# Last overflow tile of the expert stage finished apart from the other rows of a one-core decoder layer

## The chip, the cores and the metric

The kernel runs on one core of one Trainium2 chip. The metric is device time in microseconds (us), and the median of three runs before the change is 911.37 us (910.29 to 911.94). One further execution was recorded by the hardware profiler. It took 905.44 us, of which 903.5 us lie between its first and its last instruction; this stretch is called the span. All times in the tables and rows below come from that one profiled execution.

## The reference

One decoder layer over 1024 positions of width 1024: four kinds of token mixing and an output projection, then a mixture of experts with 32 experts of which each row uses two, then a plain residual add and a final RMSNorm. Only the end matters here:

```python
y = jnp.concatenate([ya, yb, yc, yd.astype(x.dtype)], axis=-1) @ w_out[l]
x = x + gt1 * y
h2 = rms_norm(x, norm2_g[l]) * (1.0 + sc2) + sh2
x = x + gt2 * hier_moe(h2, ...)       # per row: sum of two experts' outputs, each with its gate
...
return rms_norm(x, final_g)           # x * rsqrt(mean(x*x) + 1e-6) * final_g
```

An output row can be normalised only once both of its expert results are in its sum.

## The kernel before, in words

**Where the sums live.** The residual rows `x + gt1 * y` are stored in DRAM as `y_d` (1024 rows of 1024 floats, 4 KB each), and the rows that the experts read are stored as `xn2_d`. Each expert takes at most 128 rows. The table `tbl` holds, for each tile of work, a column with the row numbers of its 128 places; a place that isn't used has a number beyond the last row, and the indirect transfer leaves it out.

**Tiles.** Tiles 0 to 31 are the 32 experts in a fixed order. Rows that don't fit into their expert's 128 places go to overflow tiles 32, 33, ..., whose count `n_ov` is read from memory at run time (at least 1). With these inputs it is 1, so tile 32 is the only overflow tile. Each tile is gathered from `xn2_d` (GpSimd, `fetch`, L705), transposed by TensorE (`ex_t`), modulated by VectorE and ScalarE (`modulated`), multiplied with gate and up weights (`ex_gu`), passed through the activation (`hidden`), multiplied with the down weights (`ex_dn`), scaled by its gate into a result buffer `yo` (VectorE, `result`, L2140), and added to `y_d` by an indirect DMA that accumulates (GpSimd, `scatter_add`, L711). There are three result buffers (tile e uses `yo[e % 3]`); the overflow tile uses `yo[0]`.

**GpSimd around the end (L734 to L770).** After the scatter of tile 31 it gathers tile 33, which has no rows and is only there because each turn of the loop fetches one tile ahead. It reads `n_ov`, waits for all scatters to land (`s_sc`), and enters the overflow loop: copy the row numbers into `idx`, wait for VectorE's result (`m_yd`), start the scatter of tile 32, wait for TensorE's transposes of the next tile (`m_tx`), gather again, wait for the scatter to land, raise `ov_go`. Behind the loop it raises `f_go`.

**SyncE (L528 to L535).** It waits for `f_go`, then issues eight loads of 512 KB that bring `y_d` back into `x1[:, 0]` to `x1[:, 7]`, then eight stores to the output, each as soon as its rows are normalised (`f_o`).

**The final norm.** ScalarE squares and sums each of the eight tiles (L1356, from the last loop of its program), VectorE adds epsilon for two tiles at a time (`root_args`, L2175), GpSimd raises that to the power -0.5 (L770), and VectorE multiplies rows, factor and `final_g` (L2183, one instruction for each tile). VectorE runs `root_args` of the next pair ahead of the multiplications of a pair.

The order of the work is written out by hand; each engine runs its list in order and waits on semaphores.

Of the kernel before, what the change touches and what calls it, by code (L numbers as in the profile page):

```python
# [12 lines left out]
ALU = mybir.AluOpType  # L13
ACT = mybir.ActivationFunctionType
AX = mybir.AxisListType
ds = bass.ds
# [5 lines left out]
NT = T // P  # L22
# [92 lines left out]
def build(nc, w, out):  # L115
    ctx = ExitStack()
    with ctx:
# [3 lines left out]
        def sem(name):  # L121
            return ctx.enter_context(nc.semaphore(name))
# [126 lines left out]
        ac, o = area(REG_Y, o, 2, P)  # L249
        assert o == RES_END and o + D <= 8 * D  # L250
        fg = gtb[:, 0]

        o = RT
        rt = {}
# [89 lines left out]
        def identb(n):  # L344
# [17 lines left out]
                 "rt_pos  rt_hot far_ld rt_ld rt_n "  # L362
                 " m_tx m_xa m_xd m_gu m_th m_act m_dn m_yd "
                 "ov_w "
                 "rt_c rt_e1 rt_e2 rt_oh f_go ov_go st_x1 f_ss f_o").split()
        s = {n: sem(n) for n in names}
        s_ada = [sem(f"ld_ada{i}") for i in range(4)]
        s_win = [sem(f"ld_win{i}") for i in range(2)]
# [4 lines left out]

            return 48 * n + (16 if u >= RING - NT // 2 else 0)

        s_gx = [sem(f"gathered{i}") for i in range(BUF)]
        s_sc = [sem(f"scattered{i}") for i in range(RES)]
        s_st = [sem(f"st_xn2_{i}") for i in range(2)]
        s_fo = sem("st_out")
# [160 lines left out]
        def _(gp):  # L540
# [170 lines left out]
            def scatter_add(at, b):  # L711

                gp.indirect_dma_start(out=y_d[:, :], out_offset=bass.IndirectOffsetOnAxis(ap=at, axis=0),  # L713
                                      in_=yo[b], in_offset=None, bounds_check=last_row,
                                      oob_is_err=False, compute_op=ALU.add).then_inc(s_sc[b], 16)
# [18 lines left out]
            for e in range(3):  # L734
                gather_behind(e)
            for e in range(E):
                gp.wait_ge(s["m_yd"], e + 1)
                scatter_add(rows_of(TURN[e], 0), e % RES)
                gather_behind(e + 3)
                if e == E - 1:  # L740
                    gp.wait_ge(s["m_tx"], E + 1)
                    gather(E + 1, 0)
                if e + BUF == E:
                    gp.wait_ge(s["far_ld"], 32)
                    gp.wait_ge(s["m_tx"], E - BUF + 1)
                    gather(E, 0)
                if e == 2:
                    gp.wait_ge(s["rt_n"], 2)
                    gp.wait_ge(s["far_ld"], 16)
                if 2 <= e < 2 + 2 * NT:  # L750
                    far_scatter(e - 2)
                if e == E - 5:
                    gp.sem_inc(s["ov_go"], 1)
            n_ov = gp.value_load(idy[0:1, 0:1], min_val=1, max_val=OVT)
            for b in range(RES):
                gp.wait_ge(s_sc[b], 16 * len(range(b, E, RES)))
            with gp.Fori(0, n_ov) as i:
                ch.enter(i, 4)
                scatter_add(rows_of(i + E, 1, i + (E + 1)), 0)
                gp.wait_ge(s_gx[0], i * 16 + 16 * (E // BUF + 2))  # L760
                at = rows_of(i + (E + 2), 0, count=i + (E + 2), done="m_tx")
                fetch(at, 0)
                gp.wait_ge(s_sc[0], i * 16 + 16 * (len(range(0, E, RES)) + 1))
                gp.sem_inc(s["ov_go"], 1)
            gp.sem_inc(s["f_go"], 1)

            for i in range(NT // 2):
                gp.wait_ge(s["f_ss"], i + 1)
                at = slice(2 * i, 2 * i + 2)
                gp.tensor_tensor(rs[:, 2, at], ss[:, 2, at], mhalf[:, 0:2], ALU.pow).then_inc(s["rstd_ready"], 1)  # L770

        @block.tensor
# [580 lines left out]
        def _(act):  # L1354
# [261 lines left out]
            for j in range(NT):  # L1616
                act.wait_ge(s_w[j], w_loads(j, len(range(j, E, RING))) + 16)
                if j >= 2:
                    act.wait_ge(s["ss_ready"], 2 * NT + j - 1)
                fn(fsq[:, j % 2], x1[:, j], ACT.Square, scale=ROOT, accum_out=ss[:, 2, j:j + 1]).then_inc(s["ss_ready"], 1)  # L1620

        @block.vector
        def _(dve):
# [513 lines left out]
                stt(ac[:, par, :], a1[:, par, :], 0.5, PS[2 + par][:, P:2 * P], ALU.mult, ALU.mult).then_inc(s[pre + "act"], 1)  # L2138

            def result(e, par, pre="m_"):  # L2140
                b = e % RES if isinstance(e, int) else 0
                dve.wait_ge(s[pre + "dn"], e + 1)
                if isinstance(e, int) and e >= RES:
                    dve.wait_ge(s_sc[b], 16 * (e // RES))
                for h in range(2):
                    last = stt(yo[b][:, h * 512:(h + 1) * 512], PS[4 + 2 * par + h][:, :], gate(TURN[e] if isinstance(e, int) else e), gtb[:, 1, h * 512:(h + 1) * 512],  # L2146
                               ALU.mult, ALU.mult)
                last.then_inc(s[pre + "yd"], 1)
# [14 lines left out]
            with dve.Fori(0, n_ov) as i:  # L2163
                ch.enter(i, 1)
                hidden(i + E, 0, free=False)
                dve.wait_ge(s_sc[0], i * 16 + 16 * len(range(0, E, RES)))
                result(i + E, 0)
                modulated(xt[:, 0], i + (E + 2), "m_tx", "m_xd", 1)

            dve.wait_ge(s["xr_ld"], 16 * (NT + 1))  # L2170

            def root_args(i):
# [5 lines left out]
            for i in range(NT // 2):  # L2178
                if i + 1 < NT // 2:
                    root_args(i + 1)  # L2180
                dve.wait_ge(s["rstd_ready"], 2 * NT + i + 1)
                for j in (2 * i, 2 * i + 1):
                    stt(x1[:, j], x1[:, j], rs[:, 2, j:j + 1], fg, ALU.mult, ALU.mult).then_inc(s["f_o"], 1)  # L2183
# [24 lines left out]
```

## Time and profile before

| what | value |
|---|---|
| median of three runs | 911.37 us |
| profiled execution | 905.44 us, span 903.5 us |
| TensorE busy | 845.6 us, 94% of the span |
| VectorE / ScalarE / GpSimd busy | 455.2 / 251.7 / 277.8 us |
| data moved by the DMA engines | 136.32 MB, mean 151 GB/s |
| last TensorE instruction ends | 874.29 us |
| first load of the sums issued | 879.64 us |
| first store of the output issued | 890.64 us |

The three runs and the profiled execution differ by some 6 us, so changes are worked out inside the profiled execution and then carried over to the median. The page names a place by the line in the kernel's text; many operations are issued by small helpers, so L776 is every plain matmul and L1356 every ScalarE operation. DMA-issuing instructions on GpSimd (DMA_INDIRECT) show the time in which their descriptors are written, not the transfer. "SPq" and "POOLq" are the queues of instructions of SyncE and GpSimd.

### The profile page before, as it was taken

What the parts mean: (1) busy time and instruction counts of PE and PEld (TensorE: products, weight loads), DVE (VectorE), ACT (ScalarE), POOL (GpSimd) and SP (SyncE); (2) the same over time, 40 slices, a digit from 0 to 9 for tenths busy, and PEclk for the clock granted to TensorE, in tenths of its full rate; (3) what the DMA queues carried; (4) which work ended last, traced back from release to release, by engine and by line L of the source; (5) the groups of instructions that cost most, each with busy time, mean ns of one, the idle gap of its engine ahead of it and who ended that gap; (6) DMA issues with size and microseconds to landing.
All of it is one profiled execution on the core that took longest, in us unless ns stands there. A gap on an engine that the chain in (4) does not pass through costs nothing.

```text
span 903.5 us, 17330 instructions
## 1 busy us (share of the span) xinstructions
PE 845.6 (94%) x7134; PEld 571.5 (63%) x7134; DVE 455.2 (50%) x1145; ACT 251.7 (28%) x608; POOL 277.8 (31%) x265
## 2 busy tenths in 40 slices
PE   5999999999999999899999999999989999999960
PEld 5654445555544447688788655555788888888840
DVE  3830577766732113766674234344565555555534
ACT  5320222222200013455444112222323223223214
POOL 4810000000399500426335000000034565544242
PEclk9999999999999999999999999999999999999995
DMA  9934433444101004000000483211689999898739
GB/s 339 278 91 127 140 117 120 154 141 152 38 24 47 25 22 187 3 4 4 3 4 4 162 323 145 94 46 47 246 326 288 305 299 280 271 270 261 216 64 369
DMA packets 79637, 136.32 MB, mean 151 GB/s; under 512 B 17133, under 2 KB 51146, under 8 KB 79562
## 3 DMA queue, kind: packets, MB, share of 16 engines
q1 hardware_dynamic: 69258, 118.44, 37.8%
q0 software_dynamic: 10304, 16.82, 7.9%
q8 instruction: 55, 0.90, 0.4%
q14 instruction: 20, 0.16, 0.1%
HBM read 124.18 MB, written 29.92 MB: 171 GB/s over the span
## 4 chain that ended last, share of the span: by engine, by line
PE 88%; DVE 4%; DMA 4%; issue 2%; ACT 1%; SPq 0%; POOL 0%; DVEq 0%; POOLq 0%; ACTq 0%
PE bank L776 83%; PE bank L1308 3%; DMA REG_Y<-in_x 2%; DVE REG_P L2183 1%; DMA REG_P<-y_d 1%; PE bank L888 1%; PE bank L1239 1%; DVE REG_P L1920 1%; DMA REG_Y<-xn_d,tbl 1%; DMA y_d<-REG_Y,idx 1%; DMA y_d<-REG_Y,tbl 0%; DVE REG_P L1938 0%; ACT REG_P L1356 0%; ACT REG_W L1356 0%; PE bank L1025 0%
## 5 line engine op out<-in xcount | busy, mean ns | idle before, releaser
L776 PE MATMUL bank<-REG_W 128*128 128x512 f32 (+1 forms) x864 | 274.8, 499 | 2.5 <-DVE REG_P L1920 1.5
L776 PEld LDWEIGHTS bank<-REG_W 128*128 128x128 f32 (+1 forms) x864 | 120.9, 173 | 141.0 <-issue 136.7
L776 PE MATMUL bank<-REG_W,REG_Y 128*128 128x512 f32 x256 | 118.3, 599 | 1.4 <-DVE REG_Y L2138 1.1
L1356 ACT ACTIVATE REG_P<-bank 128x256 f32<-128x256 f32 (+2 forms) x122 | 52.7, 472 | 163.0 <-PE bank L776 134.8
L776 PE MATMUL bank<-REG_P 64*64 64x64 f32 (+1 forms) x2816 | 70.8, 228 | 8.0 <-issue 3.5
L1356 ACT ACTIVATE REG_Y<-bank,mod,s 128x128 f32<-128x128 f32 x136 | 51.1, 456 | 86.2 <-PE bank L1308 86.2
L776 PEld LDWEIGHTS bank<-REG_W,REG_Y 128*128 128x128 f32 x256 | 45.6, 191 | 44.3 <-issue 44.2
L776 PEld LDWEIGHTS bank<-REG_P 64*64 64x64 f32 x2816 | 62.9, 138 | 15.4 <-issue 5.2
L776 PEld LDWEIGHTS bank<-REG_Y,REG_W 128*128 128x128 f32 (+1 forms) x640 | 65.7, 181 | 7.2 <-issue 7.2
L776 PE MATMUL bank<-REG_Y,REG_W 128*128 128x128 f32 (+1 forms) x640 | 69.0, 276 | 0.3 <-DVE REG_Y L2007 0.3
L620 POOL TENSOR_TENSOR REG_P<-REG_P 128x1040 f32<-128x1040 f32 x2 | 4.8, 2384 | 187.1 <-DVE REG_P L1737 187.0
L776 PE MATMUL bank<-REG_Y,REG_P 128*128 128x128 f32 x496 | 58.2, 275 | 0.0
L776 PEld LDWEIGHTS bank<-REG_Y,REG_P 128*128 128x128 f32 x496 | 56.7, 192 | 0.8 <-issue 0.8
L1646 DVE SCALAR_TENSOR_TENSOR REG_Y<-REG_P,cc,REG_Y 128x256 f32<-128x256 f32 x112 | 54.3, 485 | 4.0
L713 POOL DMA_INDIRECT y_d<-REG_Y,tbl x22 | 34.9, 1588 | 59.9 <-DVE REG_Y L2146 59.9
L776 PE MATMUL bank<-REG_P,REG_Y 128*128 128x512 f32 x112 | 51.4, 592 | 0.0
L2007 DVE TENSOR_SCALAR REG_Y<-bank,s,mod 128x128 f32<-128x128 f32 x136 | 46.2, 402 | 2.3 <-PE bank L1308 2.3
L662 POOL TENSOR_TENSOR REG_P<-REG_P,lmask 128x512 f32<-128x512 f32 x20 | 26.7, 1345 | 62.9 <-DVE REG_P L1929 61.2
L565 POOL TENSOR_SCALAR ss<-ss 128x1 f32<-128x1 f32 x16 | 3.7, 234 | 137.6 <-ACT REG_P L1356 127.8
L2135 DVE SCALAR_TENSOR_TENSOR REG_Y<-REG_Y,bank 128x128 f32<-128x128 f32 x33 | 9.5, 287 | 70.7 <-issue 37.2
L2146 DVE SCALAR_TENSOR_TENSOR REG_Y<-bank,tbl,gtb 128x512 f32<-128x512 f32 x46 | 32.4, 747 | 19.1 <-PE bank L776 17.6
L1741 DVE TENSOR_SCALAR REG_P<-bank,om 128x512 f32<-128x512 f32 x7 | 5.3, 751 | 72.4 <-PE bank L776 72.4
(286 smaller groups left out, 1187.2 us busy)
## 6 DMA issues: line engine op xcount, KB each, us to landing
REG_P<-in_w_ada SPq DMA_DIRECT2D x18, 1024.0 KB, 6.2
REG_W<-in_w_in SPq DMA_DIRECT2D x17, 512.0 KB
REG_P<-in_moe_w_gate SPq DMA_DIRECT2D x17, 512.0 KB
REG_W<-in_moe_w_gate SPq DMA_DIRECT2D x16, 512.0 KB
REG_W<-in_moe_w_up SPq DMA_DIRECT2D x16, 512.0 KB
REG_W<-in_moe_w_down SPq DMA_DIRECT2D x16, 512.0 KB
REG_P<-in_moe_w_up SPq DMA_DIRECT2D x14, 512.0 KB
REG_P<-in_w_ada SPq DMA_DIRECT2D x3, 2048.0 KB, 12.3
```

The source lines that it names most:

```text
L662: gp.tensor_tensor(bl[:, l % 2], ab[:, :, 0, :], lmask[:, l:l + 1, :].to_broadcast([P, 8, CH]), ALU.mult)\
L713: gp.indirect_dma_start(out=y_d[:, :], out_offset=bass.IndirectOffsetOnAxis(ap=at, axis=0), in_=yo[b], in_offset=None, bounds_check=last_r ...
L776: return pe.matmul(o_, l, r, start=start, stop=stop, skip_group_check=True)
L888: last = pe.transpose(PS[4 + h // 2][:, ((h % 2) * 2 + kb) * P:((h % 2) * 2 + kb + 1) * P], sc[:, par, h, kb * P:(kb + 1) * P], ident[:, :])
L1239: last = pe.transpose(PS[4 + k // 4][:, (k % 4) * P:(k % 4 + 1) * P], strided[:, k, :], ident[:, :])
L1308: last = pe.transpose(PS[k // 4][:, (k % 4) * P:(k % 4 + 1) * P], xg[b][:, k * P:(k + 1) * P], ident[:, :])
L1356: return act.activation(o_, i_, f, **kw)
L1646: last = stt(dst, src[:, k], cc[:, k:k + 1], dst, ALU.mult, ALU.add)
L1920: return tt(dst[:, q::2].rearrange("p i a t -> p i (a t)"), PS[q][:, :].rearrange("p (i x) -> p i x", i=4), mskb(), ALU.mult)
L2007: last = ts(dst[:, k, :], PS[bank][:, (k - 4) * P:(k - 3) * P], s2[:, k:k + 1], mod[:, M_SH2 + k:M_SH2 + k + 1], ALU.mult, ALU.add)
L2135: ch.step(stt(a1[:, par, :], th[:, par, :], 1.0, PS[2 + par][:, 0:P], ALU.add, ALU.mult))
L2146: last = stt(yo[b][:, h * 512:(h + 1) * 512], PS[4 + 2 * par + h][:, :], gate(TURN[e] if isinstance(e, int) else e), gtb[:, 1, h * 512:(h ...
```

## The change

The overflow loop on GpSimd begins one tile earlier: its turn i scatters tile 31 + i, out of result buffer `yo[LAST]` with LAST = 31 % 3 = 1, and VectorE writes the result of tile 32 + i into that same buffer once the scatter of the tile ahead has landed. The scatter of the last overflow tile (tile 32) is no longer issued. `f_go` is raised when the scatters of tiles 0 to 31 have landed.

The rows of that last tile are then finished apart. GpSimd gathers them out of `y_d` into `late` (a free gather buffer), VectorE adds `yo[LAST]`, ScalarE squares and sums them between its squares of the second and the third tile, VectorE and GpSimd form the factor, and VectorE multiplies between the second and third output tile. The eight loads and stores of the other work stay as they were; they bring and write these rows too, without the last addition. When all eight stores have landed, GpSimd scatters `late` over the stored output (a plain indirect write) and waits for it.

```diff
@@ (gpsimd)
             for e in range(E):
-                gp.wait_ge(s["m_yd"], e + 1)
-                scatter_add(rows_of(TURN[e], 0), e % RES)
+                if e < E - 1:
+                    gp.wait_ge(s["m_yd"], e + 1)
+                    scatter_add(rows_of(TURN[e], 0), e % RES)
                 gather_behind(e + 3)
...
             n_ov = gp.value_load(idy[0:1, 0:1], min_val=1, max_val=OVT)
-            for b in range(RES):
-                gp.wait_ge(s_sc[b], 16 * len(range(b, E, RES)))
             with gp.Fori(0, n_ov) as i:
                 ch.enter(i, 4)
-                scatter_add(rows_of(i + E, 1, i + (E + 1)), 0)
+                scatter_add(rows_of(i + (E - 1), 1, i + E), LAST)
                 gp.wait_ge(s_gx[0], i * 16 + 16 * (E // BUF + 2))
                 at = rows_of(i + (E + 2), 0, count=i + (E + 2), done="m_tx")
                 fetch(at, 0)
-                gp.wait_ge(s_sc[0], i * 16 + 16 * (len(range(0, E, RES)) + 1))
+                for b in range(RES):
+                    if b != LAST:
+                        gp.wait_ge(s_sc[b], 16 * len(range(b, E, RES)))
+                gp.wait_ge(s_sc[LAST], i * 16 + 16 * len(range(LAST, E, RES)))
                 gp.sem_inc(s["ov_go"], 1)
             gp.sem_inc(s["f_go"], 1)
+
+            final_tile = gp.snap(n_ov + (E - 1))
+            gp.tensor_copy(idx[:, 1:2], tbl[:, ds(final_tile, 1), 0:1].rearrange("p o f -> p (o f)")).then_inc(s["late"], 1)
+            gp.wait_ge(s["late"], 1)
+            gp.tensor_tensor(junk[:, :], mhalf[:, 0:1], mhalf[:, 0:1], ALU.mult).then_inc(s["late"], 1)
+            gp.wait_ge(s["late"], 2)
+            gp.indirect_dma_start(out=late, out_offset=None, in_=y_d[:, :],
+                                  in_offset=bass.IndirectOffsetOnAxis(ap=idx[:, 1:2], axis=0),
+                                  bounds_check=last_row, oob_is_err=False).then_inc(s_gx[LATE_BUF], 16)
 
             for i in range(NT // 2):
...
+                if i == 0:
+                    gp.wait_ge(s["late"], 5)
+                    gp.tensor_tensor(rs[:, 1, 0:1], ss[:, 1, 0:1], mhalf[:, 0:1], ALU.pow).then_inc(s["late"], 1)
+            gp.wait_ge(s["late"], 7)
+            gp.wait_ge(s_fo, 16 * NT)
+            gp.indirect_dma_start(out=outd[:, :], out_offset=bass.IndirectOffsetOnAxis(ap=idx[:, 1:2], axis=0),
+                                  in_=late, in_offset=None, bounds_check=last_row,
+                                  oob_is_err=False).then_inc(s_late, 16)
+            gp.wait_ge(s_late, late_before + 16)
@@ (scalar, the final squares)
                 if j >= 2:
                     act.wait_ge(s["ss_ready"], 2 * NT + j - 1)
+                if j == 2:
+                    act.wait_ge(s["late"], 3)
+                    fn(fsq[:, 0], late, ACT.Square, scale=ROOT, accum_out=ss[:, 1, 0:1]).then_inc(s["late"], 1)
+                    act.wait_ge(s["late"], 4)
@@ (vector)
             def result(e, par, pre="m_"):
-                b = e % RES if isinstance(e, int) else 0
+                b = e % RES if isinstance(e, int) else LAST
...
-                dve.wait_ge(s_sc[0], i * 16 + 16 * len(range(0, E, RES)))
+                dve.wait_ge(s_sc[LAST], i * 16 + 16 * len(range(LAST, E, RES)))
                 result(i + E, 0)
                 modulated(xt[:, 0], i + (E + 2), "m_tx", "m_xd", 1)
-
+                dve.wait_ge(s["m_yd"], i + (E + 1))
+
+            dve.wait_ge(s_gx[LATE_BUF], late_before)
+            tt(late, late, yo[LAST], ALU.add).then_inc(s["late"], 1)
...
+                if i == 0:
+                    dve.wait_ge(s["late"], 4)
+                    ts(ss[:, 1, 0:1], ss[:, 1, 0:1], EPS, None, ALU.add).then_inc(s["late"], 1)
+                if i == 1:
+                    dve.wait_ge(s["late"], 6)
+                    stt(late, late, rs[:, 1, 0:1], fg, ALU.mult, ALU.mult).then_inc(s["late"], 1)
                 dve.wait_ge(s["rstd_ready"], 2 * NT + i + 1)
```

**GpSimd at the entry of the overflow loop.** In the kernel before, its list runs like this. `REG_Y` holds the result and gather buffers, a DMA with `tbl` takes the row numbers of a fixed tile and one with `idx` those of a loop turn, `m_yd` is VectorE's result and `scattered0` to `scattered2` are the landings of the scatters.

```order
L713 DMA y_d<-REG_Y,tbl 1024x1024 [waits m_yd] x2
L707 DMA REG_Y<-xn_d,tbl 128x1024 [waits m_tx]
L754 TENSOR_LOAD idy
L754 ISA x2
L757 UNCONDITIONAL_BRANCH [waits scattered2,scattered1,scattered0]
L757 ISA
L696 COPY idx<-tbl 128x1
L99 ISA
L698 REGISTER_ALU [waits chain_pool]
L689 TENSOR_TENSOR junk<-mhalf 128x1 [waits m_yd]
L713 DMA y_d<-REG_Y,idx 1024x1024
```

At the same place the changed kernel has this.

```order
L717 DMA y_d<-REG_Y,tbl 1024x1024 [waits m_yd]
L711 DMA REG_Y<-xn_d,tbl 128x1024 [waits m_tx]
L759 TENSOR_LOAD idy
L759 ISA x2
L760 UNCONDITIONAL_BRANCH
L760 ISA
L700 COPY idx<-tbl 128x1
L99 ISA
L702 REGISTER_ALU [waits chain_pool]
L693 TENSOR_TENSOR junk<-mhalf 128x1 [waits m_yd]
L717 DMA y_d<-REG_Y,idx 1024x1024
```

One of the two fixed scatters (that of tile 31) is gone from the head, the wait for all scatters is gone from the branch into the loop, and the last row is now the scatter of tile 31 and no longer that of tile 32. The gather of tile 33 stands ahead of the scatter of tile 31 now.

**GpSimd from the gather in the loop to the end.** Before, `f_ss` being VectorE's argument for the power:

```order
L707 DMA REG_Y<-xn_d,idx 128x1024
L763 REGISTER_ALU
L757 REGISTER_ALU [waits scattered0]
L757 COMPARE_AND_BRANCH
L770 TENSOR_TENSOR rs<-ss,mhalf 128x2 [waits f_ss] x4
L117 UNCONDITIONAL_BRANCH
```

After the change, `late` being the counter of the steps on the rows done apart and `st_out` that of the stores of the output:

```order
L760 REGISTER_ALU [waits scattered1]
L760 COMPARE_AND_BRANCH
L774 ISA
L774 COPY idx<-tbl 128x1
L776 TENSOR_TENSOR junk<-mhalf 128x1 [waits late]
L778 DMA REG_Y<-y_d,idx 128x1024 [waits late]
L785 TENSOR_TENSOR rs<-ss,mhalf 128x2 [waits f_ss]
L788 TENSOR_TENSOR rs<-ss,mhalf 128x1 [waits late]
L785 TENSOR_TENSOR rs<-ss,mhalf 128x2 [waits f_ss] x3
L791 DMA out_dram<-REG_Y,idx 1024x1024 [waits st_out,late]
L117 UNCONDITIONAL_BRANCH [waits gathered1_then_late_rows_stored]
```

Behind the loop stand a copy, a small multiplication and the gather out of `y_d`; one power more stands between the first and second; and the list ends with a DMA to the output that waits for the stores.

**ScalarE at the final squares.** After the change the third to fifth rows of this list are the ones around the new square, which reads `REG_Y` (`late`) while the others read `REG_P` (`x1`); `ld_expert2` is by then the landing of the load of the third tile.

```order
L1380 ACTIVATE REG_W,ss<-REG_P 128x1024 [waits ld_expert0]
L1380 ACTIVATE REG_W,ss<-REG_P 128x1024 [waits ld_expert1]
L1380 ACTIVATE REG_W,ss<-REG_Y 128x1024 [waits late,ss_ready,ld_expert2]
L1380 ACTIVATE REG_W,ss<-REG_P 128x1024 [waits late]
L1380 ACTIVATE REG_W,ss<-REG_P 128x1024 [waits ss_ready,ld_expert3]
L1380 ACTIVATE REG_W,ss<-REG_P 128x1024 [waits ss_ready,ld_expert4]
```

The square of `late` stands in the program behind the load of the third tile and in front of that tile's square, so the square of the third tile and all behind it wait for it.

## Rows read from the trace of the kernel before

**Rows 1.** The page, chain that ended last, shares of the span by engine.

```profile
PE 88%; DVE 4%; DMA 4%; issue 2%; ACT 1%; SPq 0%; POOL 0%; DVEq 0%; POOLq 0%; ACTq 0%
```

**Rows 2.** Timeline, 861 to 880 us: start us, us busy, engine, line, what [idle before].

```profile
864.38 1.56 POOL L713 DMA_INDIRECT y_d<-REG_Y,tbl  x1 [3.97 <-DVE REG_Y L2146]
...
867.04 1.56 POOL L713 DMA_INDIRECT y_d<-REG_Y,tbl  x1 [1.10 <-DVE REG_Y L2146]
868.91 1.06 POOL L707 DMA_INDIRECT REG_Y<-xn_d,tbl  x1 [0.30 <-issue]
...
870.55 1.96 PE L776 MATMUL bank<-REG_W,REG_Y 128*128 128x512 f32 x4 [1.10 <-DVE REG_Y L2138]
...
872.76 1.41 DVE L2146 SCALAR_TENSOR_TENSOR REG_Y<-bank,tbl,gtb 128x512 f32<-128x512 f32 x2 [2.36 <-PE bank L776]
...
873.20 1.09 PE L1308 MATMUL bank<-ident,REG_Y 128*128 128x128 f32 x8 [0.69 <-DMA REG_Y<-xn_d,tbl]
...
874.60 1.60 POOL L713 DMA_INDIRECT y_d<-REG_Y,idx  x1 [0.16 <-issue]
875.67 0.74 POOL L696 COPY idx<-tbl 128x1 int32 x1
...
876.84 1.09 POOL L707 DMA_INDIRECT REG_Y<-xn_d,idx  x1
879.64 3.69 SPq L531 DMA_DIRECT2D REG_P<-y_d  x8
```

**Rows 3.** Chain of waits in order of time: start us, us, what.

```profile
873.02 0.04 POOLq L757
...
874.60 4.73 DMA y_d<-REG_Y,idx
```

**Rows 4.** Timeline, from the square of the third tile to the end.

```profile
886.80 1.06 ACT L1356 ACTIVATE REG_W<-REG_P 128x1024 f32<-128x1024 f32 x1 [1.13 <-DMA REG_P<-y_d]
...
888.07 1.06 ACT L1356 ACTIVATE REG_W<-REG_P 128x1024 f32<-128x1024 f32 x1
...
889.33 2.48 DVE L2183 SCALAR_TENSOR_TENSOR REG_P<-REG_P,rs,gtb 128x1024 f32<-128x1024 f32 x2
...
890.64 8.97 SPq L534 DMA_DIRECT2D out_dram<-REG_P  x8
...
894.31 0.17 DVE L2175 TENSOR_SCALAR ss<-ss 128x2 f32<-128x2 f32 x1
894.38 4.87 DVE L2183 SCALAR_TENSOR_TENSOR REG_P<-REG_P,rs,gtb 128x1024 f32<-128x1024 f32 x4
```

**Rows 5.** Instructions of the line that reads the count of overflow tiles.

```profile
L754 POOLq TENSOR_LOAD <-idy x1: 1595/1595/1595, 866.8 to 866.8; - x1
```

**Rows 6.** DMA activity, 874.5 to 880 us: GB/s in 40 equal slices, then packets.

```profile
GB/s 0 0 0 0 0 0 0 0 0 0 0 0 0 0 0 0 179 33 1 0 30 0 30 0 30 149 30 90 60 62 60 0 1 0 1 0 0 0 0 0
DMA packets 288, 0.10 MB, mean 19 GB/s; under 512 B 263, under 2 KB 263, under 8 KB 288
```

**Rows 7.** Chain of waits at the first gather of the expert stage.

```profile
659.70 4.94 DMA REG_Y<-xn_d,tbl
```

**Rows 8.** Timeline: a scatter, the gather of tile 32, and TensorE's weight loads that waited for it.

```profile
852.66 1.56 POOL L713 DMA_INDIRECT y_d<-REG_Y,tbl  x1 [4.60 <-DVE REG_Y L2146]
854.53 1.06 POOL L707 DMA_INDIRECT REG_Y<-xn_d,tbl  x1 [0.31 <-issue]
...
862.50 0.86 PEld L1308 LDWEIGHTS bank<-ident,REG_Y 128*128 128x128 f32 x8 [0.68 <-DMA REG_Y<-xn_d,tbl]
```

**Rows 9.** DMA activity, 880.4 to 902.8 us: packets, then the queue that SyncE issues to.

```profile
DMA packets 2305, 8.40 MB, mean 375 GB/s; under 512 B 256, under 2 KB 256, under 8 KB 2304
...
q1 hardware_dynamic: 2304, 8.39, 94.9%
```

**Rows 10.** Stores of the output: time from issue to landing.

```profile
DMA to landing us min/median/max: 3.6/3.7/3.8
```

**Rows 11.** Groups of instructions on GpSimd: the plain indirect write.

```profile
L719 POOL DMA_INDIRECT far_d<-rowd,far_at x16 | 16.5, 1033 | 4.9 <-issue 4.9
```

More of the change, by code:

```diff
@@ L251, in build @@
         fg = gtb[:, 0]
+        LAST = (E - 1) % RES
+        late = xg2[:, 1]
+        LATE_BUF = 1
         o = RT
@@ L364, in build @@
                  "ov_w "
-                 "rt_c rt_e1 rt_e2 rt_oh f_go ov_go st_x1 f_ss f_o").split()
+                 "rt_c rt_e1 rt_e2 rt_oh f_go ov_go st_x1 f_ss f_o late").split()
         s = {n: sem(n) for n in names}
@@ L374, in w_loads @@
             return 48 * n + (16 if u >= RING - NT // 2 else 0)
-        s_gx = [sem(f"gathered{i}") for i in range(BUF)]
+        s_gx = [sem(f"gathered{i}" + ("_then_late_rows_stored" if i == LATE_BUF else "")) for i in range(BUF)]
+        s_late, late_before = s_gx[LATE_BUF], 16 * (len(range(LATE_BUF, E, BUF)) + 1)
         s_sc = [sem(f"scattered{i}") for i in range(RES)]
```

## The prediction

> **What bounds the kernel now.** I read the shares of the chain of waits first: TensorE holds 88% of it [rows 1], but the change touches nothing of TensorE's list, so the question is what stands behind TensorE's last work. The timeline of the last 40 us answers that. TensorE's product for tile 32 ends at 872.51 (870.55 + 1.96), VectorE's result at 874.17, the scatter of tile 32 starts at 874.60, and the first load of the sums is issued at 879.64 [rows 2]. The chain shows what lies between: 4.73 us from the scatter's start to its landing, then 0.3 us of loop end and semaphores [rows 3]. From there the tail is a pipeline with four members: loads, ScalarE's squares (one each 1.27 us: 886.80 to 888.07), VectorE's multiplications (4 in 4.87 us) and stores [rows 4]. Its DMA engines are 94.9% busy for 22 us [rows 9]. The reader is to see that the path goes: scatter landed, +7.16 us to the square of the third tile (886.80), +9.69 to the first multiplication (889.33), +19.61 to the end of the last one (894.38 + 4.87 = 899.25), +3.7 for the last store [rows 4, 10], and 0.55 to the span's end.
>
> **Part 1: the loads start earlier.** They no longer wait for the scatter of tile 32, but for three other things, and the latest of them counts.
> (a) The scatter of tile 31. It moves behind the gather of tile 33, the reading of the count and the loop's entry. The reading takes 1.6 us, but it began at 866.8, before the scatter ahead of it had even started on GpSimd at 867.04 [rows 2, 5]: the queue runs ahead of the engine, so I cost it at nothing. On the engine: the scatter of tile 30 ends at 865.94, 0.30 gap, 1.06 gather, copy 0.2 (876.20, where the DMA_INDIRECT ahead of it ends, to 876.41), and 0.43 from the copy's end to the next DMA (876.41 to 876.84) give 867.95 against 867.04, so 0.9 later [rows 2]. Before, it was landed at 873.02 [rows 3], 6.0 us after its start, with the scatter of tile 30 still ahead of it; now it lands between 872.7 (4.73 after its start) and 873.9 (6.0 after).
> (b) TensorE's transposes of the empty tile 33 (`m_tx`), for which GpSimd waits in the loop ahead of `f_go`. They waited for the gather until 873.20; that gather now runs 2.7 us earlier, so they follow the product at 872.55 and end at 873.65 [rows 2].
> (c) The steps from there to the load: dispatch 0.35, loop end 0.3. Loads at 874.3 from (b), 874.2 at the latest from (a). I take **T = 874.3, a gain of 5.3 us**. Ends: 873.6 and 875.8, the latter if the reading of the count is not covered (third rival). VectorE's result of tile 32 now waits for (a) too, to 873.9 instead of 872.76, and ends at 875.3; the list behind it waits for the late rows anyway, so this costs nothing.
>
> **Part 2: the late rows stand in ScalarE's list.** GpSimd: the empty gather 874.0 to 875.1, copy 0.2, two semaphore steps with the small multiplication 0.65; the gather of the late rows starts at T + 1.65. How long does an indirect transfer beside full queues take? The nearest rows: 4.73 us for tile 32's own 25 rows (288 packets less 263 small ones, 0.10 MB) with nothing beside it [rows 3, 6]; 4.94 us for the first gather, issued while weight loads ran [rows 7]; 8.0 us for the gather of the same 25 rows, with an accumulating scatter issued 1.9 us ahead of it (854.53 to 862.50, when TensorE's wait for it ended) [rows 8]. I take 4.9, the row with nothing accumulating ahead of it, and keep 8.0 as one end. The other end is 2.8: data began 2.1 us after the scatter's start and the counter rose 0.5 us after the last data; with the data in one burst that is what is left [rows 6]. So the rows land at T + 6.55. The addition has no row; the multiplication over the same 1024 columns takes 1.24 (2.48 for two) [rows 4], between 1.0 and 1.3 bounds it. Sum ready at T + 7.8, squared by T + 9.1 (1.27). The square of the third tile began at +7.16 and now begins at +9.1: 1.95 later. VectorE's new epsilon step, 0.17 [rows 4], stands ahead of the first multiplication. **Together 2.1 us** (ends: 1.45 where the sum is ready before the third load, since the square of the late rows is in front all the same; 5.2 with 8.0). What lies behind on ScalarE is six squares, and all of VectorE's multiplications and the stores wait for them.
>
> A rule of the Trainium skill bears on this gather: "DMA: Bandwidth & Descriptors", section "Queues, rings and completion order", says that each DMA engine takes turns between the queues it has work for, a packet at a time. By it the 25 rows wait only for about as many packets of the loads as they have themselves, which would make 4.9 a better guess than 8.0; in the row with 8.0 they waited far longer. The sum stays with 4.9 on the strength of the rows.
>
> **Part 3: VectorE has one multiplication more.** It stands between the second and the third tile. VectorE was never idle between 889.33 and 899.25, so all of it counts: **1.2 us**. The extra power on GpSimd (0.7 to 1.7 us) lies beside the two multiplications ahead of it. Cover for parts 2 and 3 could be the DMA engines' backlog: at 94.9% they were as good as a bound too. But loads of 4.2 MB at 375 GB/s, begun about 0.9 after issue, last until +12.1, and the first store is now ready at +9.7 + 2.1 + 1.24 = +13.0, so the engines run dry, and VectorE sets the pace.
>
> **Part 4: the scatter at the end.** All of it is on the path: it starts when the eighth store has landed, and nothing is behind it but the end. A plain indirect write has descriptors in 1.03 us against 1.60 for the accumulating one [rows 2, 11]; 4.73 less that 0.57 is 4.15, as nothing else is in the queues then. **Taken 4.1 us**, ends 2.8 (as above) and 4.9.
>
> **Sum.** -5.3 + 2.1 + 1.2 + 4.1 = +2.1 us in the profiled execution: span 905.6, its time 907.5. The median of the runs is 5.9 us above the profiled time; the same difference gives 911.4 + 2.1 = **913.5 us**. In words: a landing of 4.7 us is taken away in front of the tail and one nearly as long put behind it, and the later start of the pipeline's third member and one more multiplication turn the balance.
>
> **Rivals.**
> 1. *The indirect transfers are short (2.8 us)*. Then the late rows are ready before the third load, part 2 is 1.45 and part 4 is 2.8: -5.3 + 1.45 + 1.2 + 2.8 = +0.2, **911.6 us**. For it: the late rows are few, and the final write reads no sums. Against: both rows that I have for an indirect transfer of known landing say 4.7 and more.
> The Trainium skill's page "DMA: Bandwidth & Descriptors", section "Anatomy of one DMA — SWDGE (gpsimd) path", gives a fit of 2.0 us plus bytes at 436 GB/s: 2.2 us for 0.10 MB, by which the sum would be -0.4 us. The trace of this case disagrees, with 4.73.
> 2. *The late gather is slow (8.0 us)* beside eight loads at once. Part 2 is 5.2, part 4 maybe 4.7: -5.3 + 5.2 + 1.2 + 4.7 = +5.8, **917.2 us**. For it: the row with 8.0 is of the same 25 rows. Against: it had an accumulating scatter ahead of it.
> 3. *The loads don't start at 874.3*, since the reading of the count and the loop's entry now stand in front of the scatter of tile 31 and are not covered: scatter at 869.5, landed at 875.5, T = 875.8. Gain 3.8 instead of 5.3: **915.0 us**.
> 4. *The tail is bound by bytes, and the kernel is faster.* If the DMA engines' backlog carries over from loads to stores, parts 2 and 3 cost nothing and only the start and the end count: -5.3 + 0.3 (0.1 MB more) + 2.8 = -2.2, **909.2 us**. It decides if the loads' data lasts beyond the first store, that is if the first multiplication comes within about 10.9 us of T. For it: 94.9%. Against: part 2 alone moves it to +11.8, and VectorE was without a gap as well.
>
> **How the numbers follow.** Forecast 0.47, first rival 0.23, second 0.15, third 0.08, fourth 0.07. The measurement tells a change from none at about 0.2%, 1.8 us. The forecast's +2.1 lies close to that; a third of its chance goes to "same". Slower 0.31 + 0.15 + 0.08 and a little of the first rival = 0.57; same 0.35; faster 0.08. The range reaches from just below the first rival to just above the second: 911.0 to 917.3.
>
> **What the changed profile would show.** The first load at 874.3, 0.65 after the transposes end (part 1). The square of `REG_Y` starting behind a wait on VectorE's addition and not on a load, and the third tile's square 9.1 us after the first load (part 2). Nine multiplications without a gap, 11.1 us (part 3). A DMA_INDIRECT to the output once the last store has landed, and 4 us from it to the end (part 4). I am wrong if the late rows are there before the third load, if DMA engines stay full between loads and stores, or if the final write lands in under 3 us.

## The result, and the profile after

The changed kernel takes 921.56 us (median of four runs, 919.29 to 922.47), the kernel before 910.83 (four runs, 909.16 to 911.94): a ratio of 1.0116, with a 95% interval of 1.0081 to 1.0151. It is slower, as forecast, but by 10.7 us and not by 2.1, and outside the range of 911.0 to 917.3. Three executions in the chip's slower state (929.72 us of late_last_nodrain, 1283.29 of b_nodrain, 1765.02 of early_only) are left out of every median and ratio.

The profiled executions are farther apart, 920.7 us of span against 903.5. Part of this isn't the change. To take it out I count from an event ahead of it, TensorE's transposes of tile 32. They start at 862.50 before [rows 8] and 870.05 after, so 7.55 us of the 17.2 have gone by before any changed instruction runs. One stretch of 100 us ahead of it, before and then after (columns: stretch, its length, busy us of each engine with instructions, granted TensorE clock, DMA share, GB/s):

```profile
400.00:500.00 100.00, 94.39 (x2642) 81.97 (x2645) 61.28 (x120) 47.63 (x123) 44.59 (x32) 0.98 0.02 4
```
```profile
400.00:500.00 100.00, 94.11 (x2459) 81.58 (x2461) 59.48 (x117) 46.43 (x123) 44.46 (x32) 0.94 0.01 3
```

With the same code the granted clock was 0.94 of full speed in this stretch instead of 0.98, and TensorE did fewer instructions in it. The 31 runs of the kernel before on another chip spread from 903.4 to 915.2 us. The stretch from the transposes of tile 32 to the end is what the change touches: **41.0 us before, 50.65 after, +9.65**. All experiments below are read by it, and by the stretch behind the first load. Kernels with the same code between the transposes and the first load differ there by 0.5 us, so smaller differences of single traces say nothing.

The end of the changed kernel in its timeline (start us, us, engine, line, what, [idle before and what ended it]) answers to [rows 2, 4]:

```profile
870.05 1.10 PE L1332 MATMUL bank<-ident,REG_Y 128*128 128x128 f32 x8 [0.34 <-DMA REG_Y<-xn_d,tbl]
...
875.38 1.61 POOL L717 DMA_INDIRECT y_d<-REG_Y,idx  x1 [0.45 <-issue]
...
879.55 1.04 PE L1332 MATMUL bank<-ident,REG_Y 128*128 128x128 f32 x8
...
881.32 1.41 DVE L2174 SCALAR_TENSOR_TENSOR REG_Y<-bank,tbl,gtb 128x512 f32<-128x512 f32 x2 [3.71 <-DMA y_d<-REG_Y,idx]
...
881.62 3.77 SPq L535 DMA_DIRECT2D REG_P<-y_d  x8
...
883.26 1.05 POOL L778 DMA_INDIRECT REG_Y<-y_d,idx  x1 [0.28 <-POOL junk L776]
...
890.85 1.22 DVE L2200 TENSOR_TENSOR REG_Y<-REG_Y 128x1024 f32<-128x1024 f32 x1 [6.84 <-DMA REG_Y<-y_d,idx]
...
892.19 1.06 ACT L1380 ACTIVATE REG_W<-REG_Y 128x1024 f32<-128x1024 f32 x1 [4.46 <-DVE REG_Y L2200]
...
895.73 2.47 DVE L2220 SCALAR_TENSOR_TENSOR REG_P<-REG_P,rs,gtb 128x1024 f32<-128x1024 f32 x2
...
897.03 10.04 SPq L538 DMA_DIRECT2D out_dram<-REG_P  x8
...
898.19 1.28 DVE L2217 SCALAR_TENSOR_TENSOR REG_Y<-REG_Y,rs,gtb 128x1024 f32<-128x1024 f32 x1
...
910.63 1.05 POOL L791 DMA_INDIRECT out_dram<-REG_Y,idx  x1 [6.96 <-DMA out_dram<-REG_P]
```

The reader is to see three things: the loads start 11.57 us after the transposes (17.14 before [rows 2, 8]); ScalarE idles 4.46 us in front of the square of the late rows, the row that reads `REG_Y`; and the last instruction with work starts at 910.63, yet the span ends at 920.7.

What stands in those last 10 us no group of engine rows shows, since it isn't work. The chain of waits gives the first half (start us, us, what), and the instructions of the line that closes the program the second (queue, operation, duration ns three times, first and last start us):

```profile
906.73 3.04 DMA out_dram<-REG_P
909.77 0.02 issue
909.80 0.02 POOLq L790
909.82 0.81 issue
910.63 1.05 POOL out_dram L791
```
```profile
L117 POOLq COMPARE_BRANCH  x1: 41/41/41, 913.3 to 913.3; - x1
L117 POOLq DRAIN  x1: 7018/7018/7018, 913.5 to 913.5; - x1
...
L117 SPq EVENT_SEMAPHORE  x1: 17/17/17, 920.7 to 920.7; - x1
```

```profile
L117 POOLq DRAIN  x1: 8654/8654/8654, 894.5 to 894.5; - x1
...
L117 SPq COMPARE_BRANCH  x1: 37/37/37, 903.1 to 903.1; - x1
```

That drain began at 894.5 while the last power still ran, until 896.2, and ended at 903.15, 6.9 us behind it; SyncE's last wait was over at 903.1. VectorE's closing drain (3.04 us from 896.3) ended at 899.3, with its last multiplication (899.25), and not 7 us behind it.

GpSimd has one more drain, at the start of the program, and that one is short (changed kernel):

```profile
L2235 POOLq DRAIN  x1: 173/173/173, 0.4 to 0.4; - x1
```

So the 7 us don't belong to the instruction as such. No run here shows what GpSimd has done in between that makes its closing drain long.

### The profile page after: what moved, and what is told of

Its sections match the earlier page's. It is cut to its first block, busy times and chain, and to the rows that moved or that the text cites. A ratio compares the mean times of both kernels' runs of the same rounds, so it can differ in the third digit from the quotient of the medians.

```text
span 920.7 us, 17342 instructions
## 1 busy us (share of the span) xinstructions
PE 852.4 (93%) x7134; PEld 576.9 (63%) x7134; DVE 457.2 (50%) x1148; ACT 252.3 (27%) x610; POOL 279.2 (30%) x269
## 4 chain that ended last, share of the span: by engine, by line
PE 86%; DVE 4%; DMA 4%; issue 3%; ACT 1%; POOL 1%; SPq 0%; DVEq 0%; POOLq 0%; ACTq 0%
PE bank L800 81%; PE bank L1332 3%; DMA REG_Y<-in_x 2%; DMA REG_Y<-xn_d,tbl 1%; DVE REG_P L2220 1%; DMA REG_Y<-y_d,idx 1%; PE bank L912 1%; PE bank L1263 1%; DVE REG_P L1948 1%; POOL y_d L717 1%; ACT REG_W L1380 0%; DMA out_dram<-REG_P 0%; ACT REG_P L1380 0%; PE bank L1049 0%; DVE REG_P L1966 0%
## 5 line engine op out<-in xcount | busy, mean ns | idle before, releaser
L800 PE MATMUL bank<-REG_W 128*128 128x512 f32 (+1 forms) x864 | 278.2, 504 | 2.5 <-DVE REG_P L1948 1.5
L800 PE MATMUL bank<-REG_P 64*64 64x64 f32 (+1 forms) x2816 | 73.3, 235 | 8.2 <-issue 3.7
L800 PEld LDWEIGHTS bank<-REG_P 64*64 64x64 f32 x2816 | 65.7, 145 | 15.3 <-issue 5.5
```

Of the source, the lines that this page charges most:

```text
L800: return pe.matmul(o_, l, r, start=start, stop=stop, skip_group_check=True)
```

## The experiments

Two theories compete for the new time at the end: D, the closing drain costs 7 us whenever GpSimd finishes last; W, the write itself is slow and the drain only waits for it. Two more are about the late squares: S, they wait for VectorE's sum, which waits for a slow gather, and C, the gather is slow since the loads share its DMA engines. In the table "head" is from the transposes of tile 32 to the first load, "tail" from there to the end, in one profiled execution each.

| kernel | head | tail | sum | runs, median | before on that chip | ratio (95%) |
|---|---|---|---|---|---|---|
| before | 17.1 | 23.9 | 41.0 | 910.83 | | |
| changed | 11.6 | 39.1 | 50.7 | 921.56 | 910.83 | 1.0116 (1.0081-1.0151) |
| a_nodrain | 12.1 | 32.6 | 44.7 | 915.19 | 911.04 | 1.0041 (1.0005-1.0077) |
| late_last_nodrain | 11.9 | 27.6 | 39.5 | 908.52 | 911.04 | 0.9988 (0.9952-1.0023) |
| b_nodrain | 16.9 | 23.7 | 40.5 | 911.76 | 911.04 | 1.0019 (0.9988-1.0051) |
| b_poolwait | 16.7 | 31.0 | 47.7 | 919.49 | 911.04 | 1.0089 (1.0060-1.0117) |
| late_last | 12.1 | 35.4 | 47.5 | 915.41 | 910.84 | 1.0060 (1.0038-1.0082) |
| early_only | 12.0 | 24.1 | 36.2 | 905.97 | 910.84 | 0.9952 (0.9930-0.9973) |
| a_loads_held | 16.9 | 35.6 | 52.5 | 925.25 (one) | 910.84 | |
| a_nowrite | 11.7 | 35.8 | 47.5 | 917.10 (one) | 910.84 | |
| late_last_paired | 11.9 | 28.0 | 40.0 | 910.18 | 911.08 | 0.9991 (0.9968-1.0013) |

**a_nodrain: the changed kernel without GpSimd's drain.** The engines now meet by semaphores alone, and TensorE waits for the last empty gather.

```diff
-        block = ctx.enter_context(nc.Block())
+        block = ctx.enter_context(nc.Block(no_gpsimd_drain=True))
...
                 ex_t(i + (E + 1), 0, i * 16 + 16 * (E // BUF + 2))
+                pe.wait_ge(s_gx[0], i * 16 + 16 * (E // BUF + 3))
```

> The changed kernel, with the program's closing barrier built from semaphores alone, so that GpSimd does not drain at the end; TensorE waits for the last empty gather in its place. Theory D (GpSimd's closing drain of 7.0 us, from 913.5 to 920.5 in the changed kernel's trace, is what the final write newly exposes): the stretch from the last store's landing to the end shrinks from 10.9 us to about 3.9, the stretch from the transposes of tile 32 to the end from 50.65 to 43.6, and the runs come out near 914.5 us. Rival W (the final write itself is slow, and the drain only waits for it): the drain goes but the end stays, 921 us within noise.

Measured: tail 32.6 instead of 39.1; the last store landed at 910.25 and the end is at 914.2. In its list of the closing line GpSimd's queue has no drain (those of the other engines are still there):

```profile
L117 POOLq EVENT_SEMAPHORE  x2: 17/17/17, 914.0 to 914.0; - x2
...
L117 POOLq COMPARE_BRANCH  x1: 41/41/41, 913.8 to 913.8; - x1
```

Theory D holds and W falls: from the last store's landing to the end it is 3.95 us (3.9 expected) instead of 10.9. The sum of head and tail is 44.7 and not the expected 43.6; the rest lies ahead of the stores, 0.5 in the head and 0.5 in the first multiplication, whose late gather took 8.03 us here.

**b_poolwait: the drain made late in the kernel before.**

```diff
             for i in range(NT // 2):
                 ...
                 gp.tensor_tensor(rs[:, 2, at], ss[:, 2, at], mhalf[:, 0:2], ALU.pow).then_inc(s["rstd_ready"], 1)
+            gp.wait_ge(s_fo, 16 * NT)
```

> The kernel before, with one wait added at the end of GpSimd's list: for all eight stores to land. No instruction and no transfer follows it. Theory D in its strong form (the drain takes its 7 us from the moment at which GpSimd's list ends, whatever ran last): the stretch from the transposes of tile 32 to the end grows from 41.0 to 48 us, the runs to 918 us. Rival Q (the drain is long only if GpSimd has started a transfer or computed shortly before): GpSimd has been idle for 7 us by then, the drain takes under 1 us, and the time stays at 911 to 912 us.

```profile
L117 POOLq COMPARE_BRANCH  x1: 41/41/41, 906.9 to 906.9; - x1
L117 POOLq DRAIN  x1: 6937/6937/6937, 907.1 to 907.1; - x1
```

Nothing ran on GpSimd for the 7 us ahead of this drain, no transfer of it was issued for 25, and it still took 6.94 us: sum 47.7 against the expected 48, ratio 1.0089. One wait and no work costs 6.7 us in the trace, most of the change's loss. This is the strong form of D; rival Q is out.

**b_nodrain: the kernel before without the drain.** The same two edits in the kernel before.

> The kernel before, without GpSimd's closing drain (TensorE waits for the last empty gather in its place). Before, the drain ran from 894.5 to 903.15 beside the stores, whose landing SyncE saw at 903.1. Theory D: the drain was hidden, but only just, so 0 to -0.3 us: same. Rival (the drain already set the end of the kernel before): a gain of more than 0.5 us in the stretch from the transposes of tile 32 to the end, now 41.0 us.

The sum is 40.5 against 41.0, the tail 23.7 against 23.9, the ratio 1.0019 (0.9988 to 1.0051): no difference that can be told. The drain was hidden there, with next to nothing to spare. The sum's 0.5 is outside the 0 to 0.3 expected and just at the rival's bound; 0.3 of it is in the head, in which the drain has no part.

**a_nowrite: the changed kernel without the final write**, so the rows of the last overflow tile keep values without that tile's part. The wait for the stores stays.

```diff
             gp.wait_ge(s["late"], 7)
             gp.wait_ge(s_fo, 16 * NT)
-            gp.indirect_dma_start(out=outd[:, :], ...).then_inc(s_late, 16)
-            gp.wait_ge(s_late, late_before + 16)
```

> The changed kernel without the final write (the late rows keep their values without the last expert's part), but with GpSimd's wait for the stores. Theory D (write and drain are one behind the other and independent): from the first load to the end 39.1 - 3.5 (0.8 dispatch, 2.7 transfer) = 35.6 us. Rival (the drain waits for GpSimd's own last transfer, so without one it shrinks): 29 to 31 us.

```profile
L117 POOLq DRAIN  x1: 6937/6937/6937, 908.0 to 908.0; - x1
```

Tail 35.8 (35.6 expected); the drain is 6.94 us without a write and 7.02 behind one. So the end of the changed kernel splits into three that add up: 0.8 us until the write starts, 2.7 for the write, 7.0 for the drain.

**late_last_nodrain: the late rows' steps moved back as well.** GpSimd's power for the late rows moves behind its other powers and VectorE's epsilon step for them to its last pair; of the rest the edit reads:

```diff
@@ (scalar)
-                if j == 2:
-                    ...
...
+            act.wait_ge(s["late"], 3)
+            act.wait_ge(s["ss_ready"], 3 * NT - 1)
+            fn(fsq[:, 0], late, ACT.Square, scale=ROOT, accum_out=ss[:, 1, 0:1]).then_inc(s["late"], 1)
@@ (vector)
-            dve.wait_ge(s_gx[LATE_BUF], late_before)
-            tt(late, late, yo[LAST], ALU.add).then_inc(s["late"], 1)
             ...
                 for j in (2 * i, 2 * i + 1):
                     stt(x1[:, j], ...)
+                if i == 0:
+                    dve.wait_ge(s_gx[LATE_BUF], late_before)
+                    tt(late, late, yo[LAST], ALU.add).then_inc(s["late"], 1)
+            dve.wait_ge(s["late"], 6)
+            stt(late, late, rs[:, 1, 0:1], fg, ALU.mult, ALU.mult).then_inc(s["late"], 1)
```

> As the run without the drain, and in addition the late rows' steps are moved back: their addition behind the first two multiplications on VectorE, their square behind the eighth tile's on ScalarE, their multiplication last on VectorE. Theory S (the slow gather of the late rows holds up the shared squares): the first multiplication returns from 14.1 to about 9.7 us after the first load; from the transposes of tile 32 to the end 50.65 - 7.0 (drain) - 4.4 + 0 = 39.2 us, against 41.0 in the kernel before, so about 909 us, faster than both. Rival (the squares were late since loads and gather shared the DMA engines, not since ScalarE waited for VectorE's sum): the first multiplication stays at 12 us or more and the whole near 42 us, 912 or more.

```profile
880.24 3.72 SPq L535 DMA_DIRECT2D REG_P<-y_d  x8
...
887.38 1.06 ACT L1380 ACTIVATE REG_W<-REG_P 128x1024 f32<-128x1024 f32 x1 [1.19 <-DMA REG_P<-y_d]
...
889.91 2.48 DVE L2214 SCALAR_TENSOR_TENSOR REG_P<-REG_P,rs,gtb 128x1024 f32<-128x1024 f32 x2
```

The third square starts 7.14 us after the first load and the first multiplication 9.67 after, as in the kernel before (7.16 and 9.69 [rows 2, 4]), with the same gather still in flight beside them. Theory S holds: what held the squares was the order of the work around the late rows, not shared DMA engines. The sum is 39.5 us (39.2 expected). It beats the changed kernel by 11 us; against the kernel before the trace says 1.5 us less, and the ratio 0.9988 (0.9952 to 1.0023) can't tell it from no change.

The edit moves two things at once, ScalarE's square and VectorE's addition. In the changed kernel the addition stood ahead of the epsilon step of the first pair as well, so VectorE's own list waited for the gather too. Before, and then changed:

```profile
885.77 0.17 DVE L2175 TENSOR_SCALAR ss<-ss 128x2 f32<-128x2 f32 x1 [10.07 <-ACT REG_W L1356]
```
```profile
891.99 0.16 DVE L2206 TENSOR_SCALAR ss<-ss 128x2 f32<-128x2 f32 x1
892.24 0.73 POOL L785 TENSOR_TENSOR rs<-ss,mhalf 128x2 f32<-128x2 f32 x1 [7.93 <-DVE ss L2206]
```

The first pair's factor was ready at 892.97, 11.35 us after the first load, so an estimate from these rows is that moving the square alone would still leave the first multiplication 1.7 us later than before. No run moved one without the other.

**late_last: the same with the drain.**

> The changed kernel with the late rows' steps moved back (addition behind the first two multiplications, square behind the eighth tile's, multiplication last), the drain kept. Theory (drain 7.0 us and held-up squares 4.4 us are separate and add up): from the first load to the end 39.1 us in the changed kernel; here 27.6 us, as in the run with the same steps and no drain, plus 7.0 = 34.6. Rival (the drain is longer or shorter depending on what GpSimd did last): more than 0.7 us off. Runs near 916 us.

```profile
L117 POOLq DRAIN  x1: 7018/7018/7018, 906.0 to 906.0; - x1
```

Tail 35.4 us, 0.8 more than expected, which is the rival's mark. But its drain is as long as the changed kernel's; the 0.8 lies ahead of it, where the fourth square waited for its load and the first multiplication came 10.37 us after the first load instead of 9.67. The drain adds up; the 0.7 in the pipeline's start is a difference of two single traces.

**early_only: nothing but the early loads.** All steps on the late rows are left out, and with them the last overflow tile's part of the output.

> The changed kernel without any step on the late rows: the last overflow tile's contribution is left out of the output. It measures part 1 alone. Theory: the first load comes 5.0 to 5.6 us earlier, counted from the transposes of tile 32, the pipeline behind it is as before, 23.9 us, and nothing is at the end: from the transposes of tile 32 to the end 35.5 to 36 us against 41.0, runs near 906. Rival (loads that start while VectorE and GpSimd still work are slower, or the drain, which before ended 0.05 us from the stores' landing, now shows): over 36.5.

```profile
881.48 3.72 SPq L535 DMA_DIRECT2D REG_P<-y_d  x8
...
891.31 2.48 DVE L2190 SCALAR_TENSOR_TENSOR REG_P<-REG_P,rs,gtb 128x1024 f32<-128x1024 f32 x2
```

Head 12.0, tail 24.1, sum 36.2 us; ratio 0.9952 (0.9930 to 0.9973). The sum lies between the 36 of the theory and the 36.5 of the rival, nearer to the theory; the drain, 8.57 us from 896.5, again ends within 0.2 us of the stores. What the change was able to take is there: 4.9 us in the trace, 4.4 by the ratio. The steps for the late rows give back more.

**a_loads_held: the gather alone.** `f_go` is raised when the late rows have landed.

```diff
-            gp.sem_inc(s["f_go"], 1)
...
             gp.indirect_dma_start(out=late, ...).then_inc(s_gx[LATE_BUF], 16)
+            gp.wait_ge(s_gx[LATE_BUF], late_before)
+            gp.sem_inc(s["f_go"], 1)
```

> The changed kernel with the eight loads held back until the gather of the late rows has landed. It measures that gather with nothing beside it. Theory C (7.6 us in the changed kernel, since its packets share the queues with the loads): issue to landing falls to 3 us or less, like the final write (2.7). Rival (the gather is slow by itself, reading rows that a scatter has just written): it stays over 5 us.

```profile
884.61 3.27 DMA REG_Y<-y_d,idx
```

It lands in 3.27 us against 7.56 in the changed kernel. That is over theory C's bound of 3 us and far under the rival's 5: the rival of slow rows is out, and more than half of the gather's 7.56 us comes of the loads beside it. Holding the loads back for it is no remedy, the head grows to 16.9 us.

**late_last_paired: an attempt to go below both.** As late_last_nodrain, and VectorE multiplies the first two tiles as soon as their factor is there, with `root_args` of the next pair behind them.

```diff
             for i in range(NT // 2):
-                if i + 1 < NT // 2:
-                    root_args(i + 1)
                 ...
                 for j in (2 * i, 2 * i + 1):
                     stt(x1[:, j], ...)
+                    if 1 <= i < 3 and j == 2 * i:
+                        root_args(i + 1)
                 if i == 0:
+                    root_args(1)
                     ... the addition of the late rows ...
```

> The run with the late rows' steps moved back and no drain, in which moreover VectorE multiplies the first two tiles as soon as their own factor is ready, and works out the next pair's argument behind them instead of ahead. Theory B (from the first load to the last store the stretch is bound by bytes: 23.7 us with multiplications from 9.7 us on): the first multiplication moves to 7.1 us after the first load, the last store lands only 0.3 to 0.8 us earlier, at 22.9 to 23.4; from the first load to the end 26.8 to 27.3 us against 27.6, from the transposes of tile 32 to the end near 39 us against 41.0 in the kernel before: 909 us, 0.2% faster than the kernel before and 1.3% than the changed one. Rival (VectorE's start sets the end): the last store lands 2 us earlier or more, 907 us.

```profile
898.62 1.67 POOL rs L785
900.29 0.02 issue
900.31 1.28 DVE REG_P L2212
...
902.82 3.83 DMA out_dram<-REG_P
906.65 0.03 issue
```

The first multiplication came 7.18 us after the first load, and still the last store landed at +24.1, 0.4 later than without the edit. The rival (VectorE's start sets the end) is out. Theory B's gain of 0.3 to 0.8 isn't there either: the chain shows each pair's power on GpSimd, 1.6 to 1.7 us, now between VectorE's multiplications, which the old order hid, and stores that land in 4.6 us (median) instead of 2.9. What makes them slower no run shows by itself; the DMA engines have no room left there (share of their time, from 8 to 20 us after the first load in steps of 4: 0.98, 1.01 and 1.03, against 1.03, 0.94 and 1.01 without the edit). Ratio 0.9991 (0.9968 to 1.0013): no better than the kernel before by any measurement here.

## Why the prediction was wrong, point by point

**Part 1, the early loads: right in mechanism and size.** Forecast 5.3 us, measured 17.14 - 11.57 = 5.6. As forecast, (b) came last: the chain of the changed kernel goes through TensorE's transposes of tile 33 to GpSimd's wait for the scatter of tile 31 (L770).

```profile
879.71 0.89 PE bank L1332 x8
...
880.74 0.19 POOL junk L693
...
881.35 0.02 POOLq L770
...
881.42 0.05 POOL REG_Y L711
```

That wait cost nothing: the scatter, started at 875.38, had already let VectorE go on at 881.32, 5.9 us later (6.0 was my upper end). It was close, and in late_last_nodrain the scatter did come last, landing 5.80 us after its start at 874.14. Two errors cancel in part: the transposes ended 10.5 us behind those of tile 32 instead of 11.15, and (c), from there to the load, took 1.03 us and not 0.65. early_only gives 5.1 for the whole part, with nothing of the late rows in it. The scatter of tile 31 started 5.3 us behind the transposes of tile 32, against 5.45 forecast and 7.0 in rival 3, which is out.

**Part 2, the late rows in ScalarE's list: mechanism right as far as it went, size wrong.** The gather started 1.64 us after the first load (1.65 forecast) and took 7.56 us, not 4.9; my upper end was 8.0. The first multiplication came at +14.11 instead of +9.69, 4.4 us for the 2.1 that I took. The choice of 4.9 was wrong: the weight loads beside that row [rows 7] were nearly done, their queue filling 73% of the DMA engines in 661 to 662, 12% in the next us and 1% in the one after, while the loads beside the late gather kept the engines 95% busy from 883 to 892. a_loads_held shows what they cost (3.27 against 7.56). The rule of the Trainium skill that I set beside it ("DMA: Bandwidth & Descriptors", section "Queues, rings and completion order", turns between queues by packet) I read as "about as many packets of the loads as it has itself". The runs show 4.3 us more, so that reading was too kind to the change. late_last_nodrain shows that it was the place of the late rows' steps that made the gather cost anything. The price was worked out along ScalarE's list alone; the addition in front of VectorE's epsilon steps held the first pair's factor as well, until 892.97.

**Part 3: right.** Nine multiplications from 895.73 to 906.72, 10.99 us against 9.92 for eight: 1.07, forecast 1.2.

**Between the last multiplication and the last landing** the changed kernel gained some 0.7 us that I hadn't in the sum: 3.04 us (906.73 to 909.77) against the 3.7 of [rows 10]. Its DMA engines had run dry between loads and stores, as part 3 said (from 895.0 to 896.8 they moved nothing, and the first store is issued at 897.03). That the last store was quicker since it met no backlog fits this; no run tests it alone. Rival 4 is out.

**Part 4, the end: the step that failed.** The final scatter "starts when the eighth store has landed, and nothing is behind it but the end." The write took 0.8 to start and 2.7 to land, 3.5 for my 4.1: that term was nearly right, though the landing is just under my lower end of 2.8 and under the 3 us that I had named as a sign of being wrong. But behind it, and behind the end of GpSimd's list in every run that kept it, stands a drain of 7.0 us, which the prediction put at nothing without a reason: its term for the end was 4.1 us and the end took 10.5. In the kernel before it lay beside the stores, so no chain of waits and no group of busy time showed it, and the prediction had no row of the closing line. b_poolwait, in which only the wait was added, shows it without any part of the change; a_nodrain takes it away.

The sum as measured: -5.6 + 4.4 + 1.1 - 0.7 + 3.5 + 7.0 = +9.7, against +9.65 in the traces. Without the drain it would have been +2.7, close to the forecast of +2.1, but by luck: part 2 cost 2.3 us more than forecast, and part 1, the last landing, the write and part 3 together 1.7 less. The runs differ by 10.7; the 1.1 beyond the traces' 9.65 is within their spread. The forecast that the kernel gets slower came true mostly through a term that wasn't in it; a_nodrain, which lacks that term, is slower by 0.4%.

As to the first rival (short transfers): it was right on the final write, at 2.7 us against its 2.8, and wrong on the gather. The fit of the Trainium skill ("DMA: Bandwidth & Descriptors", section "Anatomy of one DMA — SWDGE (gpsimd) path": 2.0 us plus bytes at 436 GB/s, as an estimate 2.2 us for 0.10 MB) comes nearer to this write and to the gather alone (3.27) than to the 4.73 of the accumulating scatter; the gather beside the loads, 7.56, is furthest from it.

## What to carry to other kernels

Before a change gives an engine the last word in a program, look at what that engine does after its last instruction: here GpSimd's closing drain took 7 us, free as long as the stores lasted 7 us longer, and fully paid as soon as GpSimd finished last. A small side task put into the middle of a shared in-order list makes that list wait for the task's slowest input; put it last, behind everything that doesn't need it. And a transfer of 25 rows beside full load queues should be priced by a row that had the same company.

## What was not expected of the hardware

- GpSimd's drain at the end: 6.94 us with 7 us of idleness ahead of it, 7.02 us behind a transfer, 8.65 us where it began 1.7 us before the engine's last instruction ended; its drain at the start of the program: 0.17 us.
- The same indirect gather of 25 rows took 3.27 us with nothing beside it and 7.56 us beside eight loads of 512 KB (8.03 in a_nodrain, with the same loads).
- A plain indirect write of these rows landed in 2.7 us, the accumulating scatter of the same rows in 4.73 [rows 3].
- From the moment its wait was met, GpSimd took 0.81 us to start the final write (909.82 to 910.63), and 0.81 or 0.82 in each other kernel that has it.
